# Three rounded passes for the memory attention's output projection, and a dense chunk's split moved around the norm

## The chip, the cores and the metric

The kernel runs on one core of a Trainium2 chip. The metric is device time in microseconds, the median of several executions. All names of engines are the profile's: PE is TensorE, PEld its loading of the stationary operand, DVE is VectorE, ACT is ScalarE, POOL is GpSimd and SP is SyncE, which here issues the transfers of the weights.

## What is computed

Two layers of a decoder trunk for 256 tokens of width 1024. Each layer has a mixer, a cross attention into a memory of 256 rows (the memory attention), and a channel network: dense SwiGLU in layer 0, the best two of eight experts in layer 1. The two parts that matter here, from the reference:

```python
def cross_attention(h, mem_n, wq, wk, wv, wo):
    q = (h @ wq).reshape(b_, s_, XA_HEADS, XA_HEAD_DIM)      # 4 heads x 128
    k = (mem_n @ wk).reshape(b_, m_, XA_HEADS, XA_HEAD_DIM)
    v = (mem_n @ wv).reshape(b_, m_, XA_HEADS, XA_HEAD_DIM)
    s = jnp.einsum('bshd,bmhd->bhsm', q, k).astype(jnp.float32) * (XA_HEAD_DIM ** -0.5)
    p = jax.nn.softmax(s, axis=-1).astype(v.dtype)
    o = jnp.einsum('bhsm,bmhd->bshd', p, v).reshape(b_, s_, XA_WIDTH)
    return o @ wo                                            # (256, 512) @ (512, 1024)

def swiglu(h, w_gate, w_up, w_down):                         # width 2816 in the dense layer
    return (jax.nn.silu(h @ w_gate) * (h @ w_up)) @ w_down

        x = x + cross_attention(rms_norm(x, norm_xa[l]), rms_norm(mem, norm_mem[l]), ...)
        h = rms_norm(x, norm_ffn[l])
        if l % 2 == 0:
            x = x + swiglu(h, ffn_w_gate[l // 2], ffn_w_up[l // 2], ffn_w_down[l // 2])
```

All inputs and outputs are fp32.

## The kernel before

Each engine's program is written out by hand in its own block; the order on an engine is the order in that block, and engines wait for each other on counting semaphores. Weights come in units of 2 MB into `ring`, three slots of SBUF that are reused; SyncE asks for the next unit when the products of the one before it in its slot are counted.

A product is made in one of two ways. `tokens_out` (L2281, its matmul is L2283) multiplies plain fp32 operands. The other way rounds: an operand is parted into a high part, a copy in the type fp32r by ScalarE, and a low part, the remainder, by VectorE (operand minus high part), and three rounded matmuls take the place of one: low x high, high x high, high x low. `split_out` (L2299, L2300, L2303) does so for projections, with `unit_split_hi` (ScalarE, L955) and `unit_split_lo` (VectorE, L1474) for the weights, in four groups of 128x1024 a unit; `split_product` (L2724 to L2726) for the channel networks.

The memory attention: TensorE makes the query projection from `xnT` (L2276), ScalarE copies it from two banks (L1271), TensorE makes the scores of four heads (L2677). For each head VectorE takes the maximum (L1936), ScalarE the exponentials (L1278), VectorE normalises (L1944), TensorE transposes (L2688), ScalarE copies (L1287), TensorE multiplies with the values (L2698), ScalarE copies the head's output into `x_oT` (L1292). When all four heads are copied, the output projection runs: four products of 128 tokens x 512 columns, each of four matmuls, into banks 0 and 1 in turn. VectorE adds each to `x` (L1973, it counts `xo_used`). From the second product on, TensorE waits after each for an addition and transposes the quarter of `x` before it (`transpose_quarter`, L2239) for the next norm. The heads' outputs are fp32.

The dense network (layer 0) has 11 chunks of 256 columns. A chunk needs four groups of gate and up weights, 128x1024 each, parted by `split_group` (ScalarE, L938) and `split_rest` (VectorE, L1467) into six buffers, and two groups of down weights. In a chunk TensorE does the four gate-and-up groups for two tiles of 128 tokens (tile 0 into bank 0, tile 1 into bank 1, 48 matmuls together), with `flip`, the transposition of the chunk before, after the first group, and then the down groups of the chunk before. So chunk 0 has nothing between its gate and up groups and those of chunk 1. When the banks are full, ScalarE takes a tanh of each tile (L1363), VectorE makes two products of it with the bank (L2077, then L2081, which counts `act_ready`); the banks are free after that. TensorE waits at a chunk's start until both tiles of the chunk before are counted. Chunks 0 and 1 are written out, the others run in a loop.

The inputs of the network are transposed and parted before the norm's factor is known; the factor (ScalarE: squares L907, logarithm and exponential L915 and L916, with a table load each) is applied in the tanh. ScalarE does this norm after it has copied the transposed input, and then the four groups of chunk 1. VectorE does chunk 0's four remainders ahead of the four additions to `x`, and chunk 1's four remainders between the norm's result and the products of chunk 0.

In layer 1 the place of chunk 0's groups is taken by the first pieces of expert 0 (`piece_hi`, L966, and `piece_lo`, L1480, 128x2048 each; two remainders ahead of the additions).

Of the kernel before, what the change touches and what calls it, by code (L numbers as in the profile page):

```python
# [7 lines left out]
def hybrid_trunk(nc: bass.Bass, x_d, mem_d, positions_d, norm_mix_d, w_in_d, a_re_d, a_im_d, log_dt_d,  # L8
# [106 lines left out]
    with ctx:  # L115
# [177 lines left out]
        x_oT = xnT[:, 0:XH, :]  # L293
# [84 lines left out]
        def unit_hi(m):  # L378
            return UNIT_HI[m]
# [8 lines left out]
        def conv_tmp(c, t):  # L388
# [52 lines left out]
        xs_ps, xs_neg, xs_exp, xs_norm, xs_tr, xs_pT, xs_o, xs_oT = (  # L441
            sem(n) for n in ("xs_ps", "xs_neg", "xs_exp", "xs_norm", "xs_tr", "xs_pT", "xs_o", "xs_oT"))
# [33 lines left out]
        SPLIT_UNITS = [U_LATE + i for i in range(NLATE)] + [U_GLU, U_GLU + 1, U_UPM, U_UPG, U_OUT, U_OUT + 1]  # L476
# [13 lines left out]
        X_H, X_M, X_G, X_MG, XS = 0, 2, 6, 6 + NT, 10 + NT  # L490
# [395 lines left out]
        def _(act):  # L886
# [53 lines left out]
            def unit_split_hi(l, j, groups):  # L940
                for i in groups:
# [13 lines left out]
                    nc.scalar.activation(unit_hi(m), unit_raw(j, i), ACT.Copy).then_inc(split_hi, 1)  # L955
# [70 lines left out]
            for l in range(DEPTH):  # L1026
# [241 lines left out]
                sum_squares(x[:, :, :], n)  # L1268
                for b in range(2):
# [35 lines left out]
                if l % 2 == 0:  # L1305

                    act.wait_ge(slot_full[0], slot_after_chunk(l, 0, 0, 0))
                    for i in range(4):
                        split_group(splits_before(l) + gu_at(0, i), gu_buf(0, i), 0, i)
# [4 lines left out]
                if l % 2 == 0:  # L1314

                    for b in range(4):
# [20 lines left out]
                if l % 2 == 0:  # L1337
# [108 lines left out]
        def _(dve):  # L1446
# [23 lines left out]
            def unit_split_lo(l, j, groups):  # L1470
                for i in groups:
                    m = FIRST_SPLIT[j] + i
                    dve.wait_ge(split_hi, unit_splits(l) + m + 1)
                    V.tensor_tensor(unit_lo(j, i), unit_raw(j, i), unit_hi(m).bitcast(F32), ALU.subtract).then_inc(split_lo, 1)  # L1474
# [53 lines left out]
            for l in range(DEPTH):  # L1528
# [514 lines left out]
                if l % 2 == 0:  # L2043
# [3 lines left out]
                    ffn_rest(3)  # L2047
                    dve.wait_ge(norm_ss, n + 1)
                    link(V.scalar_tensor_tensor(sq_rstd, rstd, 0.5, rstd, ALU.mult, ALU.mult))
                    g0 = splits_before(l)  # L2050
# [9 lines left out]
                    def chunk(c, s):  # L2060
                        head = isinstance(c, int) and c == 0
                        if head:
                            for i in range(4):
                                split_rest(gu_at(1, i) + g0, gu_buf(1, i), 1, i)
# [900 lines left out]
```

## Time and profile before

| | |
|---|---|
| median of 3 runs | 1914.48 us (1913.58 to 1914.71) |
| profiled execution, its own time | 1917.73 us |
| its span, first to last instruction | 1916.0 us |
| mean granted clock of TensorE | 0.981 of 2.4 GHz |
| TensorE busy | 1823.3 us, 95% |
| VectorE busy | 1398.0 us, 73% |
| ScalarE busy | 1005.0 us, 52% |
| GpSimd busy | 231.3 us, 12% |

The times in the rows are microseconds from the start of the span. A row of the order of time begins with its start and its length; `x8` means that eight records stand in it. In brackets stands how long the engine was idle before it and what released it. A plain fp32 matmul leaves two records, a rounded one leaves one. Matmuls overlap, so the time for one in a sequence is the distance of starts and not the length. The granted clock is a share of 2.4 GHz: 1.00 is that level, 0.50 is 1.2 GHz.

### The profile page before, as it was taken

How to read it: one execution, taken by the hardware profiler on the slowest of the kernel's cores; microseconds unless marked ns; L12 is line 12 of the kernel's file. 1: busy time of each engine (PE TensorE's matmuls, PEld its weight loads, DVE VectorE, ACT ScalarE, POOL GpSimd, SP SyncE). 2: the span in 40 equal slices, each digit the busy share in tenths (PEclk: the TensorE clock that was granted, in tenths of full speed). 3: DMA queues.
4: the chain of work that ended last, by engine and by line, in shares of the span. 5: the costliest groups of instructions: out<-in, count | busy, mean ns of one | idle time of the engine just before them, and what ended most of it. 6: DMA issues, size and time to landing. Idle time of an engine off the chain costs nothing. (4 is left out here: it accounts for less than half of the span.)

```text
span 1916.0 us, 22585 instructions
## 1 busy us (share of the span) xinstructions
PE 1823.3 (95%) x9063; PEld 1371.9 (72%) x9063; DVE 1398.0 (73%) x1627; ACT 1005.0 (52%) x1156; POOL 231.3 (12%) x227
## 2 busy tenths in 40 slices
PE   7999999998999999998999989999999999999995
PEld 5448767585888754686666668787878787878784
DVE  4798778344455349986855259898989898989895
ACT  4231545335344313244724447777777777777773
POOL 9560001010000248100010010000000000000020
PEclk9999999899999999999999979999999999999998
DMA  7333522056553433343303459999999999999992
GB/s 244 132 132 132 176 91 87 1 216 237 177 178 124 148 132 132 132 142 123 118 16 134 152 201 391 373 393 354 393 360 392 358 392 355 392 359 392 347 392 81
DMA packets 204567, 434.85 MB, mean 227 GB/s; under 512 B 6888, under 2 KB 45936, under 8 KB 204464
## 3 DMA queue, kind: packets, MB, share of 16 engines
q1 hardware_dynamic: 196464, 414.20, 59.6%
q0 software_dynamic: 5136, 17.01, 2.5%
q10 hardware_dynamic: 2864, 2.23, 0.4%
q8 instruction: 69, 1.13, 0.2%
q14 instruction: 34, 0.28, 0.0%
HBM read 422.93 MB, written 10.49 MB: 226 GB/s over the span
## 5 line engine op out<-in xcount | busy, mean ns | idle before, releaser
L1480 DVE TENSOR_TENSOR split_e<-ring,split_e 128x2048 fp32r<-128x2048 f32 x264 | 600.6, 2289 | 54.5 <-ACT split_e L966 54.3
L966 ACT ACTIVATE split_e<-ring 128x2048 fp32r<-128x2048 f32 x264 | 503.5, 1919 | 161.0 <-PE bank L2726 153.3
L2724 PE MATMUL bank<-split_e,fx_e 128*128 128x512 f32 x704 | 279.5, 397 | 2.0 <-DVE fx_e L2136 2.0
L2726 PE MATMUL bank<-split_e,fx_e 128*128 128x512 f32 x704 | 275.3, 391 | 0.0
L2725 PE MATMUL bank<-split_e,fx_e 128*128 128x512 f32 x704 | 274.8, 390 | 0.0
L2283 PE MATMUL bank<-ring,hT 128*128 128x512 f32 x448 | 199.4, 603 | 3.0 <-DVE uT L1537 3.0
L2283 PEld LDWEIGHTS bank<-ring,hT 128*128 128x128 f32 x448 | 85.2, 193 | 109.0 <-issue 109.0
L2726 PEld LDWEIGHTS bank<-split_e,fx_e 128*128 128x128 f32 x704 | 132.5, 188 | 28.4
L2724 PEld LDWEIGHTS bank<-split_e,fx_e 128*128 128x128 f32 x704 | 132.5, 188 | 28.4 <-DVE fx_e L2136 2.2
L2725 PEld LDWEIGHTS bank<-split_e,fx_e 128*128 128x128 f32 x704 | 132.8, 189 | 26.4
L2724 PE MATMUL bank<-split_e,f_actT_e 128*128 128x512 f32 x352 | 138.7, 394 | 10.2 <-DVE f_actT_e L2144 10.2
L2725 PE MATMUL bank<-split_e,f_actT_e 128*128 128x512 f32 x352 | 137.1, 389 | 0.0
L2726 PE MATMUL bank<-split_e,f_actT_e 128*128 128x512 f32 x352 | 137.0, 389 | 0.0
L2724 PEld LDWEIGHTS bank<-split_e,f_actT_e 128*128 128x128 f32 x352 | 66.1, 188 | 27.0 <-DVE f_actT_e L2144 13.8
L2354 PE MATMUL bank<-hT,ring 128*128 128x256 f32 x384 | 84.5, 381 | 0.0
L2354 PEld LDWEIGHTS bank<-hT,ring 128*128 128x128 f32 x384 | 72.5, 190 | 11.6 <-issue 2.0
L2726 PEld LDWEIGHTS bank<-split_e,f_actT_e 128*128 128x128 f32 x352 | 66.1, 188 | 13.9
L2725 PEld LDWEIGHTS bank<-split_e,f_actT_e 128*128 128x128 f32 x352 | 66.1, 188 | 13.2
L2724 PE MATMUL bank<-split_mix,fx 128*128 128x512 f32 x168 | 67.2, 400 | 3.5 <-DVE phase L2081 3.5
L1474 DVE TENSOR_TENSOR ring_r<-ring,ring_r 128x1024 fp32r<-128x1024 f32 x46 | 54.9, 1222 | 19.5 <-ACT ring_r L955 19.3
L2726 PE MATMUL bank<-split_mix,fx 128*128 128x512 f32 x168 | 66.0, 393 | 0.0
L2725 PE MATMUL bank<-split_mix,fx 128*128 128x512 f32 x168 | 65.9, 392 | 0.0
(518 smaller groups left out, 3123.4 us busy)
## 6 DMA issues: line engine op xcount, KB each, us to landing
ring<-in_moe_w_gate SPq DMA_DIRECT2D x40, 2048.0 KB, 11.3
ring<-in_moe_w_up SPq DMA_DIRECT2D x40, 2048.0 KB, 11.1
ring<-in_moe_w_down SPq DMA_DIRECT2D x40, 2048.0 KB, 11.3
ring<-in_w_in SPq DMA_DIRECT2D x28, 2048.0 KB, 7.8
ring<-in_ffn_w_gate SPq DMA_DIRECT2D x11, 1024.0 KB, 5.5
ring<-in_ffn_w_up SPq DMA_DIRECT2D x11, 1024.0 KB, 8.0
ring<-in_ffn_w_down SPq DMA_DIRECT2D x11, 1024.0 KB, 8.7
ring<-in_ssm_w_glu SPq DMA_DIRECT2D x8, 1024.0 KB, 6.2
```

The lines of the kernel that those rows point to most:

```text
L966: nc.scalar.activation(split_e[j % NBUF][:, HI, :], ring[:, s * PIECE + i * HGRP:s * PIECE + (i + 1) * HGRP], ACT.Copy).then_inc(split_hi, 1)
L1474: V.tensor_tensor(unit_lo(j, i), unit_raw(j, i), unit_hi(m).bitcast(F32), ALU.subtract).then_inc(split_lo, 1)
L1480: V.tensor_tensor(split_e[j % NBUF][:, LO, :], ring[:, s * PIECE + i * HGRP:s * PIECE + (i + 1) * HGRP], split_e[j % NBUF][:, HI, :].bitca ...
L2283: last = mm(B[bank][:, :], src[:, k, t * P:(t + 1) * P], w[:, k, n0:n0 + 512], start=k == 0, stop=k == kt - 1)
L2354: last = mm(B[t][:, (m % 2) * SEQ:(m % 2 + 1) * SEQ], w[:, k, m * P:(m + 1) * P], hT[:, k, :], start=k == 0, stop=k == KD - 1)
L2724: mm(bank, a[HI], w[HI], start=first, stop=False)
L2725: mm(bank, a[HI], w[LO], start=False, stop=False)
L2726: return mm(bank, a[LO], w[HI], start=False, stop=last_one)
```

## The change

1. The output projection of the memory attention goes the rounded way, as `split_out` does the mixer's. Its weights are parted on ScalarE after the norm of `x` and ahead of the query copies, on VectorE after the norm's factor and ahead of the first maximum; the high parts have places of their own in each layer. Each head's output is parted: ScalarE's copy is the high part `xo_hi`, VectorE makes the remainder `xo_lo` (`xa_rest`) from the bank. The first of the four products waits for each head by itself; the bank of a head is free again when the remainder is made.
2. In the dense layer the second chunk's four groups are parted in another place. On ScalarE two come ahead of the norm, one between its squares and its logarithm, one behind it. On VectorE three remainders come ahead of the norm's factor, the fourth behind the products of chunk 0.
3. At a chunk's start TensorE waits for the bank of tile 0 ahead of that tile's matmuls and for the bank of tile 1 ahead of the other's, in chunk 1 and in the loop.

```diff
+        x_r = [over("xo_hi", [P, XH, SEQ], phase_at), over("xo_lo", [P, XH, SEQ], qk_at + 4 * (6 * NT * W + 3 * D))]
+        WO_HI = [[wo_even[:, i * GRP:(i + 1) * GRP] for i in range(4)],
+                 [wo_mem[:, 0:GRP], wo_mem[:, GRP:2 * GRP], wo_gate[:, :], wo_phase[:, :]]]
...
                 sum_squares(x[:, :, :], n)
+                unit_split_hi(l, U_WO, range(4))
                 for b in range(2):
                     act.wait_ge(xk_ps, 6 * l + 4 + b + 1)
...
-                    nc.scalar.activation(x_oT[:, h, :], B[6 + h % 2][:, 0:SEQ], ACT.Copy).then_inc(xs_oT, 1)
+                    nc.scalar.activation(x_r[HI][:, h, :], B[6 + h % 2][:, 0:SEQ], ACT.Copy).then_inc(x_hi, 1)
...
+                    act.wait_ge(slot_full[1], full_at(l, 1, 1))
+                    g0 = splits_before(l)
+                    for i in range(2):
+                        split_group(gu_at(1, i) + g0, gu_buf(1, i), 1, i)
                     act.wait_ge(xo_used, 4 * (l + 1))
-                    sum_squares(x[:, :, :], n)
+                    for t in range(NT):
+                        squares(x[:, :, :], t, h_tok, ss)
+                    split_group(gu_at(1, 2) + g0, gu_buf(1, 2), 1, 2)
+                    sum_squares(x[:, :, :], n, tiles=())
                     halve_rstd(n)
+                    split_group(gu_at(1, 3) + g0, gu_buf(1, 3), 1, 3)
...
-                        if not second:
-                            gate_up_hi(c + 1 if head else c, (s + 1) % NSLOT if head else s)
+                        if not head and not second:
+                            gate_up_hi(c, s)
...
+                def xa_rest(h):
+                    dve.wait_ge(x_hi, XS * l + X_XO + h + 1)
+                    V.tensor_tensor(x_r[LO][:, h, :], B[6 + h % 2][:, 0:SEQ], x_r[HI][:, h, :].bitcast(F32),
+                                    ALU.subtract).then_inc(x_lo, 1)
+
+                unit_split_lo(l, U_WO, range(4))
                 xa_max(0)
                 xa_max(1)
                 for h in range(XH):
                     if h + 2 < XH:
                         xa_max(h + 2)
                     xa_norm(h)
+                    if h >= 2:
+                        xa_rest(h - 2)
+                xa_rest(2)
+                xa_rest(3)
...
+                    for i in range(3):
+                        split_rest(gu_at(1, i) + g0, gu_buf(1, i), 1, i)
                     dve.wait_ge(norm_ss, n + 1)
...
-                            for i in range(4):
-                                split_rest(gu_at(1, i) + g0, gu_buf(1, i), 1, i)
...
+                        if head:
+                            split_rest(gu_at(1, 3) + g0, gu_buf(1, 3), 1, 3)
...
-                pe.wait_ge(xs_oT, XH * (l + 1))
-                arrived(l, U_WO)
-                w = slot(U_WO)[:, 0:4096].rearrange("p (k w) -> p k w", w=D)
                 for i in range(4):
                     if i >= 2:
                         pe.wait_ge(xo_used, 4 * l + i - 1)
-                    tokens_out(i % 2, x_oT, i % 2, w, KW, (i // 2) * 512).then_inc(xo_ps, 1)
+                    split_out(l, U_WO, i % 2, x_r, i % 2, (i // 2) * 512, D, i == 0, i == 3,
+                              (lambda k: XS * l + X_XO + k + 1) if i == 0 else None).then_inc(xo_ps, 1)
...
                     def chunk(c):
-                        if not first_of_all(c):
-                            pe.wait_ge(act_ready, at(c, NT - 1) - NT)
...
-                            gate_up_group(g0 + gu_at(c, i), c, i, fx, B[0:2], tiles)
+                            gate_up_group(g0 + gu_at(c, i), c, i, fx, B[0:2], tiles,
+                                          (lambda t: pe.wait_ge(act_ready, at(c, t) - NT)) if i == 0 and not first_of_all(c) else None)
```

How the instructions stand on TensorE at the output projection of layer 0, before (`bank<-ring,phase` is the projection, `ident,x` a transposed quarter of `x`):

```order
L2698 MATMUL bank<-phase,gates 128x256 [waits xs_oT,xs_pT]
L2698 MATMUL bank<-phase,gates 128x256
L2283 MATMUL bank<-ring,phase 128x512 [waits slot_full2,xs_oT]
L2283 MATMUL bank<-ring,phase 128x512 x7
L2239 MATMUL bank<-ident,x 128x128 [waits xo_used]
L2239 MATMUL bank<-ident,x 128x128 x3
L2283 MATMUL bank<-ring,phase 128x512 [waits xo_used]
```

And of the change (`wo_even` is the high part of the weights, `ring_r` the low part; the pattern of three stands once for each head and product, 24 rows ahead of the transposes):

```order
L2725 MATMUL bank<-phase,gates 128x256 [waits x_lo,xs_pT]
L2725 MATMUL bank<-phase,gates 128x256
L2326 MATMUL bank<-wo_even,xo_lo 128x512 [waits x_lo,split_lo]
L2327 MATMUL bank<-wo_even,xo_hi 128x512
L2330 MATMUL bank<-ring_r,xo_hi 128x512
...
L2266 MATMUL bank<-ident,x 128x128 [waits xo_used]
L2266 MATMUL bank<-ident,x 128x128 x3
L2326 MATMUL bank<-wo_even,xo_lo 128x512 [waits xo_used]
```

The eight matmuls ahead of the first transposes have become 24, with a wait for the low part of a head ahead of each head of the first product; the wait for `xo_used` ahead of the transposes stands where it stood.

On VectorE between the last input parts of the dense network (L1964) and the first products of chunk 0 (L2077, L2081), before:

```order
L1964 SCALAR_TENSOR_TENSOR fx<-bank,params,fx 128x256 x6
L2049 SCALAR_TENSOR_TENSOR st<-st 128x2
L1467 TENSOR_TENSOR split_mix<-ring,split_mix 128x1024 x4
L2077 SCALAR_TENSOR_TENSOR phase<-phase,bank 128x256
L2081 SCALAR_TENSOR_TENSOR phase<-phase,st,bank 128x256
L2077 SCALAR_TENSOR_TENSOR phase<-phase,bank 128x256
L2081 SCALAR_TENSOR_TENSOR phase<-phase,st,bank 128x256
L2055 TENSOR_TENSOR f_actT<-bank,f_actT 128x2x128 x2
```

And of the change, the same place:

```order
L1990 SCALAR_TENSOR_TENSOR fx<-bank,params,fx 128x256 x6
L1483 TENSOR_TENSOR split_mix<-ring,split_mix 128x1024 x3
L2078 SCALAR_TENSOR_TENSOR st<-st 128x2
L2102 SCALAR_TENSOR_TENSOR phase<-phase,bank 128x256
L2106 SCALAR_TENSOR_TENSOR phase<-phase,st,bank 128x256
L2102 SCALAR_TENSOR_TENSOR phase<-phase,bank 128x256
L2106 SCALAR_TENSOR_TENSOR phase<-phase,st,bank 128x256
L1483 TENSOR_TENSOR split_mix<-ring,split_mix 128x1024
```

Three remainders have moved ahead of the norm's factor (`st<-st`), one behind the four products.

On TensorE at the start of a chunk in the loop, before:

```order
L2730 ISA [waits act_ready]
L2724 MATMUL bank<-split_mix,fx 128x512 [waits split_lo]
L2725 MATMUL bank<-split_mix,fx 128x512
L2726 MATMUL bank<-split_mix,fx 128x512
L2724 MATMUL bank<-split_mix,fx 128x512
```

And of the change:

```order
L2820 ISA [waits split_lo]
L2749 MATMUL bank<-split_mix,fx 128x512 [waits act_ready]
L2750 MATMUL bank<-split_mix,fx 128x512
L2751 MATMUL bank<-split_mix,fx 128x512
...
L2749 MATMUL bank<-split_mix,fx 128x512 [waits act_ready]
L2750 MATMUL bank<-split_mix,fx 128x512
```

The one wait for `act_ready` ahead of twelve matmuls has become two, the second ahead of the seventh.

## Rows read from the trace of the kernel before

**Rows 1.** The page, part 1: busy us, share, instructions.
```profile
PE 1823.3 (95%) x9063; PEld 1371.9 (72%) x9063; DVE 1398.0 (73%) x1627; ACT 1005.0 (52%) x1156; POOL 231.3 (12%) x227
```

**Rows 2.** Stages: length, busy (x) of PE, PEld, DVE, ACT, POOL; clock, DMA, GB/s.
```profile
478.00:482.00 4.00, 3.84 (x11) 3.09 (x12) 0.10 (x1) 0.00 (x0) 0.00 (x0) 0.62 1.04 356
490.00:650.00 160.00, 158.96 (x721) 131.37 (x720) 88.33 (x116) 68.03 (x96) 0.00 (x0) 1.00 0.43 144
1129.60:1133.00 3.40, 3.40 (x9) 2.63 (x9) 3.03 (x8) 0.14 (x1) 2.13 (x1) 0.50 0.00 0
1160.00:1880.00 720.00, 709.42 (x3224) 583.33 (x3223) 651.23 (x405) 529.59 (x370) 18.02 (x17) 1.00 1.00 373
```

**Rows 3.** TensorE in order of time, layer 0: start, us, engine, line, operation.
```profile
447.45 7.13 PE L2283 MATMUL bank<-ring,phase 128*128 128x512 f32 x16 [0.47 <-ACT phase L1292]
454.42 0.60 PE L2239 MATMUL bank<-ident,x 128*128 128x128 f32 x4
454.86 3.60 PE L2283 MATMUL bank<-ring,phase 128*128 128x512 f32 x8
458.29 0.60 PE L2239 MATMUL bank<-ident,x 128*128 128x128 f32 x4
...
463.11 0.66 PE L2239 MATMUL bank<-ident,x 128*128 128x128 f32 x4 [0.34 <-DVE x L1973]
```

**Rows 4.** TensorE in order of time, the same place in layer 1.
```profile
1089.81 7.13 PE L2283 MATMUL bank<-ring,phase 128*128 128x512 f32 x16 [0.47 <-ACT phase L1292]
1096.87 0.66 PE L2239 MATMUL bank<-ident,x 128*128 128x128 f32 x4
```

**Rows 5.** TensorE in order of time, dense chunks 0 and 1.
```profile
466.14 0.39 PE L2726 MATMUL bank<-split_mix,fx 128*128 128x512 f32 x1
...
474.30 0.39 PE L2726 MATMUL bank<-split_end,fx 128*128 128x512 f32 x1
478.16 0.79 PE L2724 MATMUL bank<-split_mix,fx 128*128 128x512 f32 x1 [3.47 <-DVE phase L2081]
...
482.36 0.60 PE L2776 MATMUL bank<-ident,phase 128*128 128x128 f32 x4
```

**Rows 6.** VectorE in order of time, layer 0.
```profile
435.71 0.69 DVE L1936 TENSOR_REDUCE st<-bank 128x2 f32<-128x512 f32 x1 [8.89 <-PE bank L2677]
...
448.37 2.36 DVE L1467 TENSOR_TENSOR split_mix<-ring,split_mix 128x1024 fp32r<-128x1024 f32 x2 [3.93 <-ACT split_mix L938]
...
452.92 0.68 DVE L1973 TENSOR_TENSOR x<-x,bank 128x512 f32<-128x512 f32 x1
...
476.32 0.42 DVE L2077 SCALAR_TENSOR_TENSOR phase<-phase,bank 128x256 f32<-128x256 f32 x1
...
477.62 0.48 DVE L2081 SCALAR_TENSOR_TENSOR phase<-phase,st,bank 128x256 f32<-128x256 f32 x1
...
492.14 0.48 DVE L2081 SCALAR_TENSOR_TENSOR phase<-phase,st,bank 128x256 f32<-128x256 f32 x1
```

**Rows 7.** VectorE in order of time, layer 1.
```profile
1096.14 0.68 DVE L1973 TENSOR_TENSOR x<-x,bank 128x512 f32<-128x512 f32 x1
```

**Rows 8.** ScalarE in order of time, layer 0.
```profile
433.82 0.60 ACT L1271 ACTIVATE phase<-bank 128x512 f32<-128x512 f32 x1 [6.31 <-PE bank L2276]
...
470.62 3.90 ACT L938 ACTIVATE split_mix<-ring 128x1024 fp32r<-128x1024 f32 x4
...
491.18 0.84 ACT L1363 ACTIVATE phase<-bank,st 128x256 f32<-128x256 f32 x2 [5.86 <-PE bank L2726]
```

**Rows 9.** SyncE's queue in order of time, layer 0.
```profile
406.72 0.37 SPq L619 DMA_DIRECT2D ring<-in_xa_wo  x1
```

**Rows 10.** Transfers issued from 400 to 420 us: size, us to landing.
```profile
ring<-in_xa_wo SPq DMA_DIRECT2D x1, 2048.0 KB, 7.6
```

**Rows 11.** TensorE in order of time, expert layer.
```profile
1128.83 0.50 PE L2724 MATMUL bank<-split_e,fx_e 128*128 128x512 f32 x1 [2.01 <-DVE fx_e L2136]
...
1884.40 0.50 PE L2724 MATMUL bank<-split_e,f_actT_e 128*128 128x512 f32 x1 [1.75 <-DVE f_actT_e L2144]
```

More of the change, by code:

```diff
@@ L376, in hybrid_trunk, with unit_hi @@
                    + [half_r(i) for i in (1, 2, 3, 4)])
-        def unit_hi(m):
-            return UNIT_HI[m]
+        x_r = [over("xo_hi", [P, XH, SEQ], phase_at), over("xo_lo", [P, XH, SEQ], qk_at + 4 * (6 * NT * W + 3 * D))]
+        wo_even = over("wo_even", [P, 4 * GRP], qk_at)
+        wo_mem = over("wo_mem", [P, 2 * GRP], hT_at + 4 * KD * SEQ)
+        wo_gate = over("wo_gate", [P, GRP], qk_at + 4 * (6 * NT * W + 4 * D))
+        wo_phase = over("wo_phase", [P, GRP], phase_at + 4 * 6 * GRP)
+        WO_HI = [[wo_even[:, i * GRP:(i + 1) * GRP] for i in range(4)],
+                 [wo_mem[:, 0:GRP], wo_mem[:, GRP:2 * GRP], wo_gate[:, :], wo_phase[:, :]]]
+        def unit_hi(l, m):
+            return UNIT_HI[m] if m < len(UNIT_HI) else WO_HI[l % 2][m - len(UNIT_HI)]
         def unit_raw(j, i):
@@ L440, in hybrid_trunk @@
         memn_ready, xk_ps, xk_sb = sem("memn_ready"), sem("xk_ps"), sem("xk_sb")
-        xs_ps, xs_neg, xs_exp, xs_norm, xs_tr, xs_pT, xs_o, xs_oT = (
-            sem(n) for n in ("xs_ps", "xs_neg", "xs_exp", "xs_norm", "xs_tr", "xs_pT", "xs_o", "xs_oT"))
+        xs_ps, xs_neg, xs_exp, xs_norm, xs_tr, xs_pT, xs_o = (
+            sem(n) for n in ("xs_ps", "xs_neg", "xs_exp", "xs_norm", "xs_tr", "xs_pT", "xs_o"))
         xo_ps, xo_used = sem("xo_ps"), sem("xo_used")
@@ L471, in experts_before @@
             return sum(experts(m) for m in range(l))
-        SPLIT_UNITS = [U_LATE + i for i in range(NLATE)] + [U_GLU, U_GLU + 1, U_UPM, U_UPG, U_OUT, U_OUT + 1]
+        SPLIT_UNITS = [U_LATE + i for i in range(NLATE)] + [U_GLU, U_GLU + 1, U_UPM, U_UPG, U_OUT, U_OUT + 1, U_WO]
         FIRST_SPLIT = {j: 4 * i for i, j in enumerate(SPLIT_UNITS)}
@@ L488, in splits_before @@
             return unit_splits(l) + UNIT_SPLITS
-        X_H, X_M, X_G, X_MG, XS = 0, 2, 6, 6 + NT, 10 + NT
+        X_H, X_M, X_G, X_MG, X_XO, XS = 0, 2, 6, 6 + NT, 10 + NT, 10 + NT + XH
         def gu_at(c, i):
@@ L1308, in _ @@
                     for i in range(4):
-                        split_group(splits_before(l) + gu_at(0, i), gu_buf(0, i), 0, i)
+                        nc.scalar.activation(split[gu_buf(0, i)][:, HI, :], raw_group(0, i), ACT.Copy).then_inc(split_hi, 1)
                 else:
@@ L2061, in chunk @@
                         head = isinstance(c, int) and c == 0
-                        if head:
-                            for i in range(4):
-                                split_rest(gu_at(1, i) + g0, gu_buf(1, i), 1, i)
-                        else:
+                        if not head:
                             second = isinstance(c, int) and c == 1
@@ L2296, in split_out @@
                     at = (k % per_group) * width + n0
-                    hi, lo = (v[:, at:at + 512] for v in (unit_hi(m), unit_lo(j, k // per_group)))
+                    hi, lo = (v[:, at:at + 512] for v in (unit_hi(l, m), unit_lo(j, k // per_group)))
                     a = [src[v][:, k, t * P:(t + 1) * P] for v in (HI, LO)]
@@ L2370, in late_gate @@
                     at = slice(t * P, (t + 1) * P)
-                    ws = [[v[:, (k % 2) * 512:(k % 2 + 1) * 512] for v in (unit_hi(FIRST_SPLIT[j] + k // 2), unit_lo(j, k // 2))]
+                    ws = [[v[:, (k % 2) * 512:(k % 2 + 1) * 512] for v in (unit_hi(l, FIRST_SPLIT[j] + k // 2), unit_lo(j, k // 2))]
                           for k in range(KD)]
@@ L2695, in x_out @@
                     if h >= 2:
-                        pe.wait_ge(xs_oT, n - 1)
+                        pe.wait_ge(x_lo, XS * l + X_XO + h - 1)
                     for m in range(NT):
@@ L2726, in split_product, with gate_up_group @@
                     return mm(bank, a[LO], w[HI], start=False, stop=last_one)
-                def gate_up_group(at, c, i, src, banks, tiles):
+                def gate_up_group(at, c, i, src, banks, tiles, bank_free=None):
                     pe.wait_ge(split_lo, at + 1)
                     w = split[gu_buf(c, i)].rearrange("p a (k n) -> p a k n", n=512)
-                    for bank, (t0, t1) in zip(banks, tiles):
+                    for n_, (bank, (t0, t1)) in enumerate(zip(banks, tiles)):
+                        if bank_free is not None:
+                            bank_free(n_)
                         for k in range(2):
```

7 lines of the change are left out of this document (3 added, 4 removed).

## The prediction

> **What bounds the kernel now.** The page's busy times come first: TensorE works 1823.3 us of the span [rows 1], so a microsecond counts where TensorE waits, or where its work gets shorter with nothing else queued in front. The table by stages shows where it does not wait: in the dense chunks from 490 to 650 us it is busy 158.96 of 160 us, in the experts 709.42 of 720 us [rows 2]. The order of time on TensorE shows the rest. In layer 0 the output projection of the memory attention runs from 447.45 us; records x16 are eight matmuls, since a plain fp32 matmul leaves two records. Four of them take 3.43 us (454.86 to 458.29), 0.857 us each [rows 3]. Layer 1 repeats it from 1089.81 us [rows 4]. Then the dense network: after its first chunk TensorE stands 3.47 us, released by VectorE L2081, the product that frees the banks [rows 5]. ScalarE and VectorE are read last, for what TensorE will meet when it comes earlier.
>
> **Part 1, the projection.** Sixteen fp32 matmuls a layer become 48 rounded ones. The price of a rounded one is that of the dense chunk: 466.14 to 474.30 us are 36 of them, 0.227 us each [rows 5]. Three take 0.680 us against 0.857 us: 16 x 0.177 = 2.8 us less work a layer. The start also moves: the old one waited 0.47 us for the last head's copy [rows 3], the new one waits head by head. It can start at 446.98 us, and needs the fourth head only 9 x 0.227 = 2.04 us later.
> The rows say that three rounded matmuls take 0.79 of one fp32 matmul. The Trainium skill, in "FP8 and Floating Point Precision", section TensorE Precision Notes, says that true fp32 is four passes through the array, which would make it 0.75. By that page the two parts that count below would save 1.72 instead of 1.42 us each, and the sum would be about 0.6 us larger. The trace does not agree, and the sum goes by its rows.
>
> What stands in front decides how much of it arrives. The first two products (24 matmuls, 5.44 us) now end at 452.42 us. The transposes behind them need VectorE's first addition to x, and VectorE does the four remainders of chunk 0 first: from 448.37 us, 1.18 us each, then the addition from 452.92 us [rows 6], done at 453.60. So the transposes start at 453.65 instead of 454.42 us [rows 3]: 0.77 us won of 1.4 + 0.47, and a new idle of some 1.0 us. Behind them nothing of that kind stands: from the first transposes to the last it took 463.11 - 454.42 = 8.69 us, in which eight fp32 matmuls (6.86 us) become 24 rounded ones (5.44 us). Gain 1.42 us. Layer 0: 2.19 us.
> In layer 1 the remainders are larger, and the first addition starts at 1096.14 us and takes 0.68 us [rows 7]; the transposes started at 1096.87 us [rows 4], so here the gate already bound. The earlier start and the first two products win nothing, the last two 1.42 us. TensorE will idle from 1089.34 + 5.44 + 0.16 (the last one's end) = 1094.95 to 1096.87, 1.9 us.
>
> What the projection's split costs: four ScalarE copies of 128x1024 (0.98 us each, from the four in 3.90 us [rows 8]) and four VectorE subtractions (1.18 us), before the query copies. Of those the second starts at 433.82 us after 6.31 us idle [rows 8], and the scores need both, so 3.9 us fit. VectorE stood 8.89 us before its first maximum [rows 6]; 4.7 us fit. The projection's weights are asked for at 406.72 us and land after 7.6 us [rows 9, 10], 12 us ahead of the copies. The four small remainders of the heads (128x256; a product of that size takes 0.48 us [rows 6]) stand behind a normalisation each, while ScalarE still has exponentials to do. I cost all this at nothing; without the cover it would be 3.9 us of ScalarE a layer.
>
> **Part 2, the seam after chunk 0.** Now: TensorE ends chunk 0 at 478.16 - 3.47 = 474.69. VectorE is busy with the four remainders of chunk 1 until 476.32, then does two products a tile, the last ending at 478.10 [rows 6]. After: three remainders lie before the norm's result, the fourth behind the gating, and the first tile's bank releases its own six matmuls. The length of the free chain is that of the next chunk: tanh starts at 491.18 [rows 8], the first tile's product starts at 492.14 and takes 0.48 [rows 6]: 1.44 us, with 0.10 us of hand-overs 1.54. Idle 3.47 becomes 1.54: gain 1.93 us. The second tile is ready 0.85 us later, while the first tile's six matmuls take 1.36 us. The fourth remainder is needed only by the last group, 8 us on.
> ScalarE keeps its work and changes its order. It ended the four copies at 474.52, 0.17 us before TensorE [rows 8]; it starts 2.2 us earlier, as TensorE does, so it stays just in time.
> Then the clock. After the 3.47 us idle the granted clock fell to 0.62 between 478 and 482 us [rows 2], between its levels 2.4 and 1.2 GHz: twelve matmuls took 482.36 - 478.16 = 4.20 us instead of 2.72 [rows 5]. An idle of 1.75 us at 1884.40 was followed by matmuls at full speed [rows 11]. With 1.54 us the clock stays: gain 1.48 us. From below: it falls all the same, gain 0.
>
> **Part 3, waits by tile in the loop.** The order shows one more wait on act_ready in the middle of each first group, against a loop's variable. The dense stretch is 1.04 us idle in 160 [rows 2], so there is nothing to win; the nearest row for such a wait is that stretch, where the one at the chunk's start costs nothing visible. I take 0.
>
> **Against it: the clock in layer 1.** The new idle of 1.9 us lies between the 1.75 us without a fall and 2.01 us at 1128.83, after which the clock was 0.50 for 3.4 us [rows 2, 11]. Such a stretch costs about 1.5 us, as above. The rows stand on both sides and equally near, so I take half, 0.8 us; the ends are 0 and 1.5.
>
> **The sum.** 2.19 + 1.42 + 1.93 + 1.48 - 0.8 = 6.2 us. The profiled execution took 1917.73 us (span 1916.0), 3.25 over the median of the runs; the change acts on both alike: 1911.5 profiled, 1914.48 - 6.2 = 1908.3 us median. The experts do not absorb it: their loads are issued when groups are freed, which moves with TensorE.
>
> **Rivals.**
> More than forecast: no fall in layer 1, and one fall of the clock elsewhere that the profiled execution had does not come, since all behind layer 0 is shifted. 7.0 + 1.5 = 8.5 us: 1906.0 us. For it: 1.75 us left the clock alone. Against it: 2.01 us did not [rows 11].
> The clock takes it back: it falls after the new 1.0 us idle of layer 0, after the seam and in layer 1: 7.0 - 3 x 1.5 = 2.5 us, 1912.0 us. For it: the same rows that fell. Against it: those idles were 2 us and longer, and 1.75 us left it alone. The Trainium skill's "TensorE: Matmul & The Clock Gate", section HAM oscillation, speaks for this one: short bursts of work between waits start at the half rate each time.
> The seam is not shortened because ScalarE comes late: its margin is 0.17 us. If its reordered norm costs 2 us more, the seam stays at 3.47 and the clock falls: 7.02 - 3.4 = 3.6 or less, within what can be told apart.
> Slower: the second wait by tile costs in every pass. TensorE is the bound there, so it is paid in full: ten chunks have it, and from (6.2 + 3.8) / 10 = 1.0 us a chunk the kernel is slower by over 0.2%: 1918.3 us. Against it: 1.04 us of idle in 160 with the same wait at the chunk's start [rows 2].
>
> **How the numbers follow.** What a measurement of this kernel can tell from no change is about 0.2%, 3.8 us. Forecast (4.5 to 7 us) 0.57; more than that 0.21; the clock takes it back 0.14; the late ScalarE 0.04; slower 0.04. Faster 0.78, the same 0.18, slower 0.04. The range leaves out the slower rival and little else: 1905.8 to 1912.2.
>
> **What the next profile shows.** Right: the projection as 48 records a layer, the first transposes some 6.7 to 7.5 us behind its start with an idle released by VectorE's addition (about 1.0 us in layer 0, 1.9 in layer 1); the idle before chunk 1's first matmul about 1.5 us instead of 3.47, twelve matmuls behind it in 2.7 us; the dense stretch as dense as before. Wrong: an idle before the query-key scores or before the projection (the splits were not covered), granted clock 0.5 behind the new idles, or idles in the middle of the loop's first groups.

## The result, and the profile after

| | executions | median us | ratio to before, 95% |
|---|---|---|---|
| before | 6 | 1914.72 (1913.58 to 1917.87) | |
| changed | 6 | 1902.85 (1899.46 to 1907.11) | 0.9942 (0.993 to 0.9954) |
| changed, profiled execution | 1 | 1899.46, span 1897.7, mean granted clock 0.988 | |

The kernel is faster by 11.9 us, where 6.2 were forecast; 1902.85 lies below the range. The two profiled spans are 18.3 us apart, more than the medians: the profile of before is of one of its kernel's longer executions, that of after of its kernel's shortest. So the pair of profiles tells where time can go, and only many executions tell how often it goes there.

TensorE in order of time, changed kernel:

```profile
443.57 0.58 PE L2326 MATMUL bank<-wo_even,xo_lo 128*128 128x512 f32 x1
...
449.01 0.39 PE L2330 MATMUL bank<-ring_r,xo_hi 128*128 128x512 f32 x1
450.61 0.66 PE L2266 MATMUL bank<-ident,x 128*128 128x128 f32 x4 [1.22 <-DVE x L1999]
...
453.87 0.60 PE L2266 MATMUL bank<-ident,x 128*128 128x128 f32 x4
...
458.02 0.66 PE L2266 MATMUL bank<-ident,x 128*128 128x128 f32 x4 [0.35 <-DVE x L1999]
...
471.29 0.47 PE L2749 MATMUL bank<-split_mix,fx 128*128 128x512 f32 x1 [1.71 <-DVE phase L2106]
...
474.14 0.60 PE L2803 MATMUL bank<-ident,phase 128*128 128x128 f32 x4
...
1083.53 0.66 PE L2266 MATMUL bank<-ident,x 128*128 128x128 f32 x4 [2.06 <-DVE x L1999]
...
1113.21 0.50 PE L2749 MATMUL bank<-split_e,fx_e 128*128 128x512 f32 x1 [2.01 <-DVE fx_e L2163]
```

Against [rows 3 to 5]: the projection's first 24 matmuls take from 443.57 to 449.39, and an idle of 1.22 us stands before the first transposes where none was; from the first transposes to the last it is 7.41 us instead of 8.69. The seam is 1.71 instead of 3.47, and the twelve matmuls behind it take 2.85 us instead of 4.20. In layer 1 the new idle is 2.06 us.

VectorE, changed kernel:

```profile
424.55 4.63 DVE L1490 TENSOR_TENSOR ring_r<-ring,wo_even 128x1024 fp32r<-128x1024 f32 x4 [0.78 <-ACT wo_even L962]
432.59 0.69 DVE L1952 TENSOR_REDUCE st<-bank 128x2 f32<-128x512 f32 x1 [3.41 <-PE bank L2704]
...
447.60 2.35 DVE L1483 TENSOR_TENSOR split_end<-ring,split_end 128x1024 fp32r<-128x1024 f32 x2
449.87 1.28 DVE L1999 TENSOR_TENSOR x<-x,bank 128x512 f32<-128x512 f32 x2
...
470.20 0.42 DVE L2102 SCALAR_TENSOR_TENSOR phase<-phase,bank 128x256 f32<-128x256 f32 x1 [1.91 <-ACT phase L1379]
470.66 0.48 DVE L2106 SCALAR_TENSOR_TENSOR phase<-phase,st,bank 128x256 f32<-128x256 f32 x1
...
1078.38 4.49 DVE L1496 TENSOR_TENSOR split_e<-ring,split_e 128x2048 fp32r<-128x2048 f32 x2 [1.51 <-ACT split_e L973]
1082.79 1.28 DVE L1999 TENSOR_TENSOR x<-x,bank 128x512 f32<-128x512 f32 x2
```

ScalarE, changed kernel:

```profile
423.41 3.88 ACT L962 ACTIVATE wo_even<-ring 128x1024 fp32r<-128x1024 f32 x4
430.77 0.60 ACT L1279 ACTIVATE phase<-bank 128x512 f32<-128x512 f32 x1 [3.00 <-PE bank L2303]
...
468.37 1.06 ACT L945 ACTIVATE split_mix<-ring 128x1024 fp32r<-128x1024 f32 x1
469.62 0.84 ACT L1379 ACTIVATE phase<-bank,st 128x256 f32<-128x256 f32 x2 [0.19 <-PE bank L2751]
```

The splits of the projection's weights are covered: ScalarE still waits 3.00 us before its query copy and VectorE 3.41 before its first maximum. The first addition stands directly behind VectorE's remainders in both layers (447.60 and 1078.38, no idle). Before the tanh at the seam ScalarE waits 0.19 us for TensorE, so it is just in time.

Windows of the changed kernel: the seam, the dense stretch, layer 1's new idle, the first expert's start.

```profile
471.00:475.00 4.00, 3.71 (x18) 3.13 (x19) 2.12 (x5) 0.45 (x2) 0.00 (x0) 1.00 0.76 256
476.00:625.00 149.00, 149.00 (x674) 123.33 (x673) 81.79 (x105) 63.19 (x88) 0.00 (x0) 1.00 0.45 153
1081.00:1087.00 6.00, 3.94 (x22) 2.97 (x21) 3.10 (x4) 0.95 (x1) 0.00 (x0) 1.00 0.01 3
1113.00:1116.50 3.50, 3.29 (x14) 2.71 (x15) 3.26 (x14) 1.12 (x1) 1.24 (x1) 1.00 0.00 0
```

The granted clock is 1.00 in all four: behind the seam, where [rows 2] had 0.62, behind the new 2.06 us idle, where half a fall was subtracted, and behind the same 2.01 us idle of the expert layer after which it was 0.50 before. That last difference is not the change's: the second profile of the kernel before (below) has no fall there either, and two of the changed versions have one.

Where the 18.3 us between the two profiles lie. The table is worked out from the traces: the same matmul is looked up in each, and the distance of two such matmuls is a stretch. The first number is its length in us, the second the time in it at a granted clock of 0.50. Names are the times of the kernel before.

```
stretch      before       changed
290-305      15.04/3.4    13.37/0
366-383      17.16/10.2   15.69/6.8
440-463      22.55/0      20.51/0      projection, layer 0
463-478      15.05/0.5    13.27/0      seam
478-484       6.01/2.9     4.67/0      behind the seam
484-670     185.94/0     185.92/0      dense chunks
670-690      20.04/6.8    18.84/3.4
925-945      20.02/3.4    18.52/0
1010-1030    20.04/3.4    18.45/0
1075-1106    30.40/3.4    27.80/0      projection, layer 1
1120-1128     8.71/6.1     7.80/4.2
1128-1136     7.20/3.4     5.61/0
1136-1860   724.18/0     724.25/0      experts
```

The edited places give 2.04 (layer 0), 1.78 (seam), 1.34 (behind it) and, against the 29.16 us of the kernel with the seam and the waits alone (below), which has layer 1's old projection without a fall, 1.36: 6.5 us. Seven stretches in which no instruction changed, and the fall in 1075-1106 (30.40 - 29.16 = 1.24), give 1.67 + 1.47 + 1.20 + 1.50 + 1.59 + 1.24 + 0.91 + 1.59 = 11.2 us, all of them with less time at the low clock. The first two of these, 3.1 us, lie ahead of every edit. TensorE starts the scores of layer 0, the last thing ahead of the new projection that the edits do not touch, that much earlier; before, then changed:

```profile
434.47 1.78 PE L2677 MATMUL bank<-gates,phase 128*128 128x256 f32 x7 [0.69 <-ACT phase L1271]
```

```profile
431.42 3.72 PE L2704 MATMUL bank<-gates,phase 128*128 128x256 f32 x16 [0.69 <-ACT phase L1279]
```

No edit to what comes later can have moved these by shifting work. The rest, some 0.6 us, is 1.00 us between 1860 and 1884 less small losses elsewhere.

### The profile page after: what moved, and what is told of

Its sections match the earlier page's. It is cut to its first block, busy times and chain, and to the rows that moved or that the text cites. A ratio compares the mean times of both kernels' runs of the same rounds, so it can differ in the third digit from the quotient of the medians.

```text
span 1897.7 us, 22679 instructions
## 1 busy us (share of the span) xinstructions
PE 1804.3 (95%) x9095; PEld 1369.5 (72%) x9095; DVE 1410.7 (74%) x1643; ACT 1012.4 (53%) x1164; POOL 228.0 (12%) x227
## 4 chain that ended last, share of the span: by engine, by line
PE 80%; DVE 11%; ACT 5%; issue 2%; DMA 1%; ACTq 0%; POOL 0%; DVEq 0%; SPq 0%
PE bank L2749 14%; PE bank L2751 14%; PE bank L2750 14%; PE bank L2310 10%; PE bank L2381 4%; DVE split_e L1496 3%; PE bank L2303 2%; PE bank L2326 2%; PE bank L2330 2%; PE bank L2327 2%; PE bank L2551 2%; DVE phase L1745 1%; PE bank L2403 1%; PE bank L2409 1%; PE bank L2405 1%
## 5 line engine op out<-in xcount | busy, mean ns | idle before, releaser
L2751 PEld LDWEIGHTS bank<-split_e,f_actT_e 128*128 128x128 f32 x352 | 66.1, 188 | 13.9
## 6 DMA issues: line engine op xcount, KB each, us to landing
ring<-in_moe_w_down SPq DMA_DIRECT2D x40, 2048.0 KB, 11.7
```

The costliest lines, as they stand in the source:

```text
L2751: return mm(bank, a[LO], w[HI], start=False, stop=last_one)
```

## The experiments

Each execution has its own mean granted clock, and the two go together: among the executions of before 1917.13 us at 0.980 and 1908.17 at 0.987. A straight line through all executions of all kernels, with one slope and a level for each kernel, gives about 1.4 us per 0.001 of clock. The table has the mean, its standard error, and the mean clock. Kernels were run in five sessions, each beside the kernel before; the first row pools the four for which every execution's clock is on record. The six executions of before in the first session average 1915.53 us. (Three executions, at 2201, 5954 and 10346 us, are left out.)

| kernel | executions | mean us | mean clock | ratio to before, 95% |
|---|---|---|---|---|
| before, four sessions | 70 | 1914.45 ± 0.31 | 0.9821 | |
| changed, both sessions | 11 | 1903.73 ± 0.73 | 0.9867 | 0.9943 (0.993 to 0.9955), second session |
| projection alone | 10 | 1908.85 ± 0.85 | 0.9852 | 0.9974 (0.996 to 0.9989) |
| seam and waits alone | 6 | 1908.32 ± 0.97 | 0.9863 | 0.9968 (0.9955 to 0.9981) |
| changed, one wait at chunk start | 5 | 1907.85 ± 0.50 | 0.9844 | 0.9964 (0.9951 to 0.9977) |
| before, again | 11 | 1913.69 ± 0.49 | 0.9832 | 0.9994 (0.9985 to 1.0003) |
| before + 4 repetitions | 11 | 1912.74 ± 0.80 | 0.9852 | 0.9992 (0.9982 to 1.0001) |
| before + 8 repetitions | 12 | 1917.49 ± 0.86 | 0.9823 | 1.0015 (1.0004 to 1.0026) |
| changed + 4 repetitions | 9 | 1906.77 ± 1.46 | 0.9864 | 0.9963 (0.9947 to 0.9979) |
| changed, addition earlier | 12 | 1901.22 ± 0.95 | 0.9856 | 0.993 (0.9913 to 0.9947) and 0.993 (0.9908 to 0.9952) |
| changed, router filled | 5 | 1902.79 ± 0.70 | 0.9880 | 0.9942 (0.9929 to 0.9955) |
| both | 5 | 1900.69 ± 1.16 | 0.9864 | 0.9932 (0.9919 to 0.9945) |

**The changed kernel again**, without an edit.

> The changed kernel itself, again, beside the others. Theory A (direct work plus clock): matmul by matmul the first pair of profiles gives 6.8 us that lie at the edited places (projection 2.16 in layer 0 and 1.56 in layer 1, seam 1.78, clock right behind the seam 1.34); all else, 11.5 us of that pair, is granted clock at places whose instructions did not change, 2.9 us of it ahead of every edit. So the executions should spread by 5 us or more, the time should follow the mean granted clock of the execution, and at equal clock the gain over the kernel before should be near 7 us. Theory B (the whole gain of 12 us is the change's own work): the place-by-place gains at the edits add to 12 us in a second profile too. Expected ratio 0.993 to 0.996 by both.

Median 1904.37 us. Its profile (span 1903.3) has the same idles at the seam (1.70 us) and in layer 1 (2.05), and a longer one in layer 0:

```profile
450.25 0.66 PE L2266 MATMUL bank<-ident,x 128*128 128x128 f32 x4 [1.70 <-DVE x L1999]
```

There ScalarE waited 0.37 us for the transfer of the first chunk's weights. VectorE's remainders and its first addition came about 0.5 us later behind the scores than in the first profile, and the projection in layer 0 won 1.56 us instead of 2.04. The stretches 670-690 and 1010-1030 are 20.06 and 20.03 us again, as before, and the low stretches in 925-945 and 1075-1106 are back too: what the first profile won there is not the edit's. The scores of layer 0 start at 430.59 us:

```profile
430.59 3.72 PE L2704 MATMUL bank<-gates,phase 128*128 128x256 f32 x16 [0.69 <-ACT phase L1279]
```

Against the second profile of the kernel before (span 1911.9, scores at 433.89 us) the difference is 8.7 us: 3.3 us lie ahead of every edit, 6.3 us at the edited places and right behind the seam, and all the rest loses 0.9 us. So in this second pair nothing was won in the untouched work behind the edits.

**The projection alone.** The edits of the seam and of the waits are undone:

```diff
-                    for i in range(3):
-                        split_rest(gu_at(1, i) + g0, gu_buf(1, i), 1, i)
                     dve.wait_ge(norm_ss, n + 1)
...
+                        if not first_of_all(c):
+                            pe.wait_ge(act_ready, at(c, NT - 1) - NT)
```

> Only the output projection in three rounded passes; the dense chunk's split and the waits for the banks as before. Theory A: direct gain 2.2 us in layer 0 and 1.4 to 1.6 us in layer 1, 3.7 us together; the seam after chunk 0 stays at 3.47 us of idle with the granted clock low behind it; on top of it comes granted clock elsewhere, between -3 and +6 us, so 1905 to 1913 us. Theory B: a fixed part of the 12 us, some 6 us, in every execution, with a spread like that of the kernel before.

Median 1908.22 us. TensorE at the seam:

```profile
472.33 0.50 PE L2740 MATMUL bank<-split_mix,fx 128*128 128x512 f32 x1 [3.48 <-DVE phase L2099]
...
473.47 0.63 PE L2741 MATMUL bank<-split_mix,fx 128*128 128x512 f32 x1
473.90 0.63 PE L2742 MATMUL bank<-split_mix,fx 128*128 128x512 f32 x1
```

The seam and its fall are back: starts 0.43 us apart instead of 0.23 from the fifth matmul on.

**The seam and the waits alone.** The same edits put into the kernel before, with its projection left as it was.

```diff
+                    for i in range(3):
+                        split_rest(gu_at(1, i) + g0, gu_buf(1, i), 1, i)
                     dve.wait_ge(norm_ss, n + 1)
...
-                        if not first_of_all(c):
-                            pe.wait_ge(act_ready, at(c, NT - 1) - NT)
```

> Only the dense chunk's split around the norm and the waits by tile; the projection in fp32 as before. Theory A: idle before chunk 1 falls from 3.47 to about 1.7 us (1.8 us won) and the clock stays up behind it (1.3 to 1.5 us won), 3.2 us direct; elsewhere up to the seam the trace is that of before but for the granted clock. 1906 to 1913 us. Theory B: some 6 us in every execution.

Median 1907.65 us.

```profile
472.22 0.47 PE L2733 MATMUL bank<-split_mix,fx 128*128 128x512 f32 x1 [1.71 <-DVE phase L2088]
```

The seam is 1.71 us with the old projection too. The halves gain 5.6 and 6.1 us by the means, together 11.7 ± 1.4, and the whole 10.7 ± 0.8: they add up, but each is 2 to 3 us more than what it changes directly (3.4; 1.78 + 1.34). In their profiles too the scores of layer 0, ahead of every edit, start early, at 430.5 and 430.3 us.

**One wait at the chunk's start.** The split around the norm stays, the wait by tile goes:

```diff
+                        if not first_of_all(c):
+                            pe.wait_ge(act_ready, at(c, NT - 1) - NT)
...
-                            gate_up_group(g0 + gu_at(c, i), c, i, fx, B[0:2], tiles,
-                                          (lambda t: pe.wait_ge(act_ready, at(c, t) - NT)) if i == 0 and not first_of_all(c) else None)
+                            gate_up_group(g0 + gu_at(c, i), c, i, fx, B[0:2], tiles)
```

> The changed kernel with one wait for both banks at a chunk's start instead of one for each tile. The idle before chunk 1 grows by the second tile's 0.85 us, from 1.7 to about 2.56 us; if the clock then falls behind it, another 1.3 to 1.5 us are lost, if not, nothing. In the loop no difference (under 0.3 us over nine passes). So 0.85 to 2.3 us slower than the changed kernel at equal clock elsewhere. If the wait by tile cost time in the loop, this kernel would be faster in the stretch of the dense chunks.

Median 1907.78 us.

```profile
473.39 0.50 PE L2749 MATMUL bank<-split_mix,fx 128*128 128x512 f32 x1 [2.46 <-DVE phase L2106]
```

Waiting by tile shortens the seam by 0.75 us; the order of the split alone by 1.02. No fall follows this idle of 2.46 us: the twelve matmuls behind it are as quick as in the changed kernel. In the loop the two are equal: from 484 to 640 us both take 156.00 us, as the kernel before does. Of the 4.1 us between the means, more than the 0.85 to 2.3 that were expected, 0.75 is seen; the rest goes with the lower mean clock.

**Work shifted, nothing else changed.** In front of the first transposed quarter of layer 0 TensorE makes the same four transposes again, into the same bank, 4 or 8 times; this is work done twice. The kernel before is run again beside them.

```diff
                         pe.wait_ge(xo_used, 4 * l + i)
+                        if l == 0 and i == 1:
+                            for _ in range(4):
+                                transpose_quarter(0)
                         transpose_quarter(i - 1)
```

> The kernel before, once more, for a second profile of it. Between the six profiles so far all stretches of TensorE agree within 0.1 us except at the edits and where the granted clock falls. Theory A1 (luck of the profiled execution, and of few executions): a second profile of before shows other low stretches than the first, and the low time outside the seam is on average like that of the changed kernel. Theory A2 (the low stretches depend on where the work lies, and the kernel before lies badly): the second profile repeats the low stretches of the first, above all the one behind 1128 us and the long one at 369 us.

> The kernel before with four repetitions of one quarter's transposition (16 transposes more) in layer 0's output projection: 1.76 us of added work on TensorE, nothing else. Output unchanged. Theory A1: 1.8 us slower than before, mean clock 0.982 to 0.983 as before. Theory A2: the clock behind that place changes by more than the work: the mean clock goes up (0.985 or more) and the time comes out equal or lower than before although work was added.

> The same with eight repetitions, 3.5 us of added work. Theory A1: 3.5 us slower than before at the same mean clock. Theory A2, with the length of a low stretch (3.4 us) as the distance at which the pattern repeats: also 3.5 us slower at the mean clock of before, unlike the kernel with four repetitions.

> The changed kernel with the same four repetitions, 1.76 us of added work. Theory A1: 1.8 us slower than the changed kernel (some 1905.5 us), mean clock near 0.986. Theory A2: the changed kernel lies well for the clock, so a shift of half the length of a low stretch takes part of it away: more than 1.8 us slower, mean clock 0.984 or lower.

Medians 1913.89, 1912.6, 1917.0 and 1905.4 us. The repetitions cost 1.74 and 3.49 us where they stand (440-463: 24.29 and 26.04 against 22.55). Yet the kernel with four of them is not slower than its own kernel; the interval ends at 1.0001, where 1.74 us would be 1.0009. With eight the time is up by 3.0 us, as the work says, and the mean clock is that of before.

The second profile of the kernel before repeats nearly all low stretches of the first, at the same work: 296, 477, 675, 938, 1013, 1081 and 1109 us. It has a shorter one at 368 us (6.8 instead of 10.2) and none at 1129 us, the two named above all in the expectation for a kernel that lies badly.

Two windows, first in the kernel before again:

```profile
1013.00:1027.00 14.00, 11.47 (x43) 7.09 (x41) 6.84 (x12) 9.13 (x12) 0.00 (x0) 0.88 0.00 1
1078.00:1090.00 12.00, 9.31 (x39) 6.65 (x38) 4.75 (x18) 8.39 (x25) 0.00 (x0) 0.86 0.82 301
```

with four repetitions:

```profile
1013.00:1027.00 14.00, 10.69 (x48) 6.60 (x48) 7.47 (x15) 9.50 (x13) 0.00 (x0) 1.00 0.00 0
1078.00:1090.00 12.00, 8.92 (x44) 6.34 (x44) 6.03 (x20) 8.49 (x25) 0.00 (x0) 1.00 0.91 341
```

and with eight:

```profile
1013.00:1027.00 14.00, 13.10 (x40) 7.07 (x40) 5.05 (x12) 6.44 (x9) 0.00 (x0) 0.63 0.00 0
1078.00:1090.00 12.00, 8.72 (x43) 6.32 (x41) 6.15 (x20) 7.31 (x22) 0.00 (x0) 1.00 0.82 292
```

The column behind POOL is the granted clock. The shift is 1.74 us and 3.49 us, and the clock 560 us later is 0.88, 1.00 or 0.63. These are single profiles, and they prove less than they seem to: the work around 1013 us took 18.45 us in one profile of the changed kernel and 20.03 in the other, with no edit between them. The three also differ ahead of the repetitions, where the scores of layer 0 start at 433.9, 434.6 and 431.7 us. So that the shift made these falls come and go is not shown by them; what speaks for it is the mean over executions. The same four repetitions in the changed kernel left its mean clock at 0.9864; with a standard error of 1.46 us this run can't tell the two theories apart.

**VectorE's first addition earlier.** It moves ahead of the last two of the four remainders in layer 0 and of the second in layer 1; its work stays the same.

```diff
                     for i in range(4):
                         split_rest(splits_before(l) + gu_at(0, i), gu_buf(0, i), 0, i)
+                        if i == 1:
+                            xo_add(0)
                 else:
                     piece_lo("g", 0, 0, 0)
+                    xo_add(0)
                     piece_lo("g", 0, 0, 1)
...
-                for i in range(4):
+                for i in range(1, 4):
```

> The changed kernel with VectorE's first addition of the projection to x ahead of the last remainders of the first chunk (layer 0) and of the first piece's second half (layer 1). Theory C (the addition queued behind the remainders is what TensorE waits for ahead of the transposes, 1.2 us in layer 0 and 2.06 us in layer 1): both idles vanish, 3.2 us won at equal mean clock, some 1900.5 us. Rival: the idle goes over to the next addition or to the first chunk's groups, and less than 1 us is won.

TensorE, first transposes of each layer:

```profile
447.67 0.60 PE L2272 MATMUL bank<-ident,x 128*128 128x128 f32 x4
...
1082.92 0.66 PE L2272 MATMUL bank<-ident,x 128*128 128x128 f32 x4
```

VectorE, the addition at its new place:

```profile
446.03 0.68 DVE L1983 TENSOR_TENSOR x<-x,bank 128x512 f32<-128x512 f32 x1
446.63 2.35 DVE L1483 TENSOR_TENSOR split_end<-ring,split_end 128x1024 fp32r<-128x1024 f32 x2
```

Both idles are gone. The stretches shrink from 20.51 to 19.08 and from 27.80 to 25.63, 3.6 us together. Median 1899.73 us. Since its six executions spread over 10.5 us, it ran once more:

> The version with VectorE's first addition moved ahead, once more, since its first six executions spread over 10.5 us. If the two idles that it removes are its whole gain (3.6 us by the profiles), the mean lies near 1903.7 - 3.6 = 1900.1 us at the same mean clock, and together with the first six it stays at least 2 us below the changed kernel's mean of 1903.7. If the first six were luck in the granted clock, the new ones lie at 1902 us or above.

Median 1902.72 us, mean 1901.37; the mean of the twelve is 1901.22, 2.5 ± 1.2 us under the changed kernel at a mean clock lower by 0.001. On the fitted line, at one clock, it is 4.1 us under it, close to the 3.6 us of the stretches. The second profile has 25.63 us again in layer 1; in layer 0 a low stretch at 438 us makes it 20.09. It is the best version of the study.

**The idle around the router filled.** From 1096 us on TensorE waits for the choice of experts, 6.46 us, with the clock at 0.50. Three useless 128x512 fp32 matmuls are put behind the router's products and one behind the five small ones:

```diff
                     last.then_inc(rl_ps, 1)
+                    for _ in range(3):
+                        mm(B[5][:, :], ident[:, :], hT[:, 0:2, :].rearrange("p k n -> p (k n)"), start=True, stop=True)
```

> The changed kernel with three matmuls of no use (fp32, 128x512, into a bank that is free) behind the router's and one behind the five small ones, in layer 1, where TensorE stands 6.5 and 1.3 us. Output unchanged. Theory D (the low clock of 13.7 us there comes of that idle and costs the gather and what follows): the gather's stretch gets 1 to 2 us shorter, the fall behind the 2.0 us idle does not come; 1.5 to 3 us won although work was added, mean clock up by 0.002. Rival: the clock stays low whatever is put there, or the matmuls delay the five small ones, and the kernel is the same or up to 1 us slower.

> Both of these. By C and D 4.5 to 6 us under the changed kernel, 1898 us or less in the median; if the two stand in each other's way, no less than the better of the two.

Medians 1903.49 and 1901.36 us. One window of the changed kernel and then of the filled one:

```profile
1093.00:1111.00 18.00, 10.29 (x62) 10.13 (x62) 7.38 (x35) 4.25 (x7) 0.00 (x0) 0.62 0.54 212
```

```profile
1093.00:1111.00 18.00, 15.76 (x69) 11.08 (x69) 8.43 (x35) 5.38 (x10) 0.00 (x0) 0.72 0.59 230
```

The low time there shrinks from 13.7 to 10.2 us, and no gain can be told from noise: 1902.79 ± 0.70 against 1903.73 ± 0.73, where 1.5 to 3 us were expected. Both edits together are no better than the earlier addition alone; 1898 us or less was expected. Most of that low time lies where TensorE waits for others (1106 to 1120 takes 14.0 us in every profile without the filling, whatever the clock, and 13.9 with it). The stretches behind it are no shorter either (1120 to 1128 takes 7.85 us, 7.80 in the changed kernel). So the theory that the low clock there costs 1.5 us or more fell.

## Why the prediction was wrong

**What held.** The terms worked out from durations, measured against forecast: projection in layer 0 2.04 (2.19), in layer 1 1.36 (1.42), the seam 1.78 (1.93), the clock behind it 1.34 (1.48); together 6.5. The projection's gain in layer 0 is not the same in every profile: with the projection alone it is 1.86, and 1.56 in the second profile of the changed kernel, in which the first chunk's weights came late. The seam is 0.17 us longer than forecast: from the tanh's start to the end of tile 0's second product it is 1.52 us (469.62 to 471.14) where 1.44 were taken, and the two hand-overs around it are 0.19 instead of 0.10. The splits are covered; ScalarE is just in time; the waits by tile cost nothing in the loop and are worth 0.75 us at the seam. The idle before the first transposes came, released by VectorE's addition, as said: 1.22 us (1.0; 1.70 in the second profile) and 2.06 (1.9), and moving the addition took it away. The rivals of a late ScalarE and of a dear wait are refuted. So is the one in which the clock takes it back: no profile has a fall right behind the new idles of 1.2 to 2.1 us. The section HAM oscillation of the Trainium skill's "TensorE: Matmul & The Clock Gate", which the prediction cites for that rival, tells of waits of about 3 to 5 us, longer than these idles.

**"I take half, 0.8 us".** Wrong: no profile with layer 1's idle of 2.05 to 2.08 us has a fall right behind it, and the term is 0. Rows with a fall (2.01 us) and without one (1.75 us) were read as a threshold in the length of the idle. The same 2.01 us idle at the first expert had a fall in the first profile of the kernel before and none in its second; 2.46 us at the seam had none, 3.48 had one.

**The step that failed: "the change acts on both alike: 1911.5 profiled, 1914.48 - 6.2 = 1908.3 us median".** It took the clock everywhere else as fixed: the sum has no term for it. Measured over many executions the gain is 10.7 us; the terms above make 6.5, and 4.2 us remain, nearly three falls of 1.5 us. The mean clock went from 0.9821 to 0.9867. The first rival came nearest ("one fall of the clock elsewhere", 1906.0 us, a chance of 0.21), but its size was a third of what came and its reason, "since all behind layer 0 is shifted", covers at most a part: in the two pairs of profiles 3.1 and 3.3 us of what was won outside the edited places lie ahead of every edit, and behind them it is 8.0 us in one pair and a loss of 0.9 in the other. That much was there to see beforehand: the kernel before had low stretches in some ten places, most in work that the change does not touch, and each could go or come.

**Shown, supported, open.** Shown: the direct terms, by stretches that repeat to 0.1 us in the profiles with the same edit, the projection in layer 0 apart (to 0.5); that the unchanged stretches differ by their time at the low clock; the idle's cause. Supported: that added work alone can change the clock elsewhere, by the run with four repetitions (a ratio whose interval leaves out the 1.0009 of their own work). Open: what the 4.2 us come from. The scores of layer 0, ahead of every edit, start at 431.7 to 434.6 us in the four profiles of kernels without the edits (mean 433.7) and at 429.9 to 432.8 in the ten with one or both of them (mean 431.4); a later edit can't shift these, and nothing here tells why they differ. Open too: why the kernel before has 0.982 in every session, and which shift is a good one; one or two profiles for each kernel don't tell how often each fall comes. Reducing all to one clock is rough too: on the fitted line the whole change is worth 4.2 us and its two halves 1.3 and 0.2, each less than its direct terms, so the line puts part of the direct gain on the clock.

## What to carry to other kernels

Before a sum is set against the median, count the places at which the granted clock was low outside the change: each of those falls may go or come at some 1.5 us apiece, ahead of the edit as well as behind it, and the range has to hold two or three of them. When TensorE's work in front of a hand-over gets shorter, look at what the engine that answers does first: here 3.6 us more were had by moving one addition in front of two splits. Compare edits of a few microseconds by many executions with their clock beside them, not by two profiles. Take two profiles of one kernel before calling a difference in untouched work the edit's.

## What the hardware showed that was not expected

- Executions of one kernel spread over some 8 us (1899.46 to 1907.11), and the time follows the mean granted clock, about 1.4 us per 0.001.
- An idle's length did not decide whether the clock fell: 2.01 us with and without, 2.06 and 2.46 without, 3.47 and 3.48 with. The 2.8 us idle before 296 us had a fall behind it in both profiles of the kernel before and in neither of the changed one, though no edit comes before it.
- 1.74 us of added work in layer 0 made the kernel no slower (0.9992, 0.9982 to 1.0001), at a mean clock of 0.9852 against 0.9832 for the kernel before beside it; 3.49 us of added work made it slower by about as much (1.0015).
- Three rounded matmuls of 128x512 took 0.68 us in the projection as in the dense chunks (0.227 us each; 446.06 to 449.01 us are 13 of them), so the price held in a place where it had not been measured.
